# One attention and mixture-of-experts block on one core: how x arrives and is scaled, and the four gate units as seven half-size products

## The chip, the cores and the metric

One NeuronCore of a Trainium2 chip runs the whole program; the other cores are idle. The metric is the device time of one execution in microseconds (us), smaller is better.

## What is computed

All data are float32. `x` is 256 tokens of width 1024. The block adds two terms to it.

```python
h = x
xn = rms_norm(h, norm_mix_g)
proj = xn @ w_in                       # 4808 columns: qa ka va qi ki wi qb kb vb ga gb
# oa: 8 heads over the 64 keys that an index score selects; ob: 8 heads of stick-breaking attention
merged = sigmoid(ga) * (oa @ w_proj_a) + sigmoid(gb) * (ob @ w_proj_b)
h = h + merged @ w_out
hn = rms_norm(h, norm_ffn_g)
# router: top 4 of 32 experts per token; each expert is 1024 -> 2 x 1024 -> 1024 with biases
h = h + sum over the chosen experts of gate * ((up + 1) * g * sigmoid(1.702 * g) @ w_down + b_down)
```

`ga` and `gb` are the two gates, 1024 columns each, so 2048 of the 4808 projected columns. The norm gain multiplies the transposed x by row, the reciprocal root of each token's mean square multiplies it by column.

## The kernel before, in words

**The engines each have one program, written out by hand.** There is no planner: the order on TensorE, VectorE, ScalarE, GpSimd and the DMA queue of SyncE is the order of the calls in the file, and semaphores tie them together. A DMA on SyncE's queue that must wait for a buffer holds all behind it.

**Projection.** `w_in` is cut into ten units (L102): QI, KI with KA, QA, QB, KB, VB, and units 6 to 9, the four gate units of 512 columns. Each is a 2048 KB load. x comes transposed (`XT`, feature chunks of 128 by 256 tokens) in three transfers of 2, 3 and 3 chunks on ScalarE's queue (L1550). VectorE multiplies chunks 0 and 1 by the gain (L1166), ScalarE chunks 2 to 7 (L1556). TensorE's `first_unit` (L652) takes chunk after chunk as they are scaled; behind its chunk 5 come two products that spread the root over the partitions (L648), for which VectorE has to square x (L1169), GpSimd to take the root (L579) and VectorE to build a diagonal from the identity (`ident`, loaded on SyncE's queue, L421), which ends with the semaphore `v_dg` (L1176). A *token half* (L615) is one block of 128 tokens by the unit's columns; a *column half* (L627) is two blocks of 128 columns by all 256 tokens: 16 products of 128x128 by 256 columns, each shown as two records. Results go to the two banks of `Pp`, and ScalarE copies each half out (`evacuate`, L1536, shown as L1544).

**Attention beside it.** Between the halves TensorE does the small products of both attentions (L755 to L796): transposes of the rotated heads (L680; they wait for `v_rota`, with which VectorE ends its normalising and rotating of the A heads, L1213 to L1233), index scores and logits (L697), and for each of four pairs of B heads `b_logits` (L705), `b_sums` (L716, waits for VectorE's `b_softplus`, L1273 and L1276), `b_values` (L725, waits for ScalarE's `b_exp`). The column halves of units 6 to 9 stand between these as work that needs neither VectorE nor GpSimd. `turn_probabilities` (L742) waits for VectorE's `normalise` (L1267).

**GpSimd** does little: a root of 18 numbers per partition (L579), a cast (L587), the router's weights times the gain (L590), all around 50 us, and two more roots later.

**Loads around it.** SyncE loads unit u when the half that frees its buffer is done (L444). Two buffers of 2048 KB (`unit`) serve most units; `w_proj_a`, `w_proj_b` and the two halves of `w_out` are units 10 to 13. Then, after the last attention results (L504), come the first pieces of experts 0 and 1, and after them the experts in order, two experts' places deep, each piece waiting for the release by TensorE (L462).

**After the gates** TensorE multiplies by `w_proj_a` and `w_proj_b` (L809), VectorE merges (L1320), then `w_out` (L820), the router (L837) and 32 experts (L913 to L955), each 12 MB of weights.

Of the kernel before, what the change touches and what calls it, by code (L numbers as in the profile page):

```python
# [21 lines left out]
ALU = mybir.AluOpType  # L22
# [82 lines left out]
GAINS = 5 * KC  # L105

# [30 lines left out]
def hybrid_block(nc, x, xt, w_in, gain_rows, head_rows, w_proj_a, w_proj_b, w_out,  # L137
                 w_router, w_gate_up, b_gate_up, w_down, b_down, consts, out):
    with ExitStack() as ctx:
# [62 lines left out]
        KD = G[:, 0, :, :]  # L202
        RT = OAT[:, 0:3, :]
# [56 lines left out]
        in_xt = [sem(f"in_xt{i}") for i in range(3)]  # L260
# [11 lines left out]
        m_half, a_half = sem("m_half"), sem("a_half")  # L272
        v_roti, v_rota = sem("v_roti"), sem("v_rota")
# [24 lines left out]
        def uview(u, n=512):  # L298
            flat = slot(2, 0, 4096) if u == 2 else unit[:, u % 2, :]
            return flat[:, 0:8 * n].rearrange("p (k n) -> p k n", k=8)  # L300

        def urows(u):

            flat = unit[:, 0, :] if u == 10 else slot(4, 0, 4096)
            return flat.rearrange("p (k n) -> p k n", k=4)

# [97 lines left out]
        def _(sp):  # L404
# [16 lines left out]
            sp.dma_start(ident, consts[:, C_ID:C_ID + P]).then_inc(in_id, 16)  # L421
# [178 lines left out]
        def _(pe):  # L600
# [51 lines left out]
            def first_unit():  # L652

                for k in range(KC):
                    if k < 2:
                        pe.wait_ge(v_xt, k + 1)
                    else:
                        pe.wait_ge(a_xt, k - 1)
# [11 lines left out]
                nhalf[0] = 2  # L670

# [101 lines left out]
            column_half(6, 0)  # L773
# [3 lines left out]
            column_half(6, 1)  # L777
            b_sums(1)
            column_half(7, 0)
# [3 lines left out]
            column_half(7, 1)  # L783
# [3 lines left out]
            column_half(8, 0)  # L787
            b_values(2)
            b_logits(3)
            column_half(8, 1)  # L790
            b_sums(3)
            turn_probabilities(0, 2)
            column_half(9, 0)
            b_values(3)
            a_values(0, 2, 2)
            column_half(9, 1)  # L796
# [4 lines left out]
            for c in range(KC):  # L801
                if c >= 2:
                    pe.wait_ge(v_mg, c - 1)
                else:
                    pe.wait_ge(a_half, nhalf[0] - 1 + c)
# [27 lines left out]
            def router_products(b, i):  # L833

                pe.wait_ge(a_xt, 7 + 2 * b + i)
# [278 lines left out]
        def _(dve):  # L1114
# [49 lines left out]
            dve.wait_ge(in_xt[0], 16)  # L1164
            for k in range(2):
                V.tensor_scalar(XT[:, k, :], XT[:, k, :], g_mix[:, k:k + 1], None, ALU.mult).then_inc(v_xt, 1)  # L1166
# [80 lines left out]

            def select_keys(b, nk):
# [55 lines left out]
            out_of_bank(m_pt, 1, W2, Ap[:, :, :].rearrange("p a n -> p (a n)"), v_pt)  # L1304
            b_softplus(2)
            b_argument(2)
            out_of_bank(m_pv, 1, OAT[:, :, P:SEQ], Ap[:, 0, :].rearrange("p (j q) -> p j q", j=NP2), v_pv)
            mask_logits(0, P, Ap[:, 2:4, :].rearrange("p a (j s) -> p (a j) s", j=NP2), 2)
            b_softplus(3)
            normalise(P, 2)  # L1310
            b_argument(3)
            out_of_bank(m_pt, 2, W2[:, 0:1024], Ap[:, 0:2, :].rearrange("p a n -> p (a n)"), v_pt)
            out_of_bank(m_pv, 2, OAT[:, :, 0:P], Ap[:, 2, :].rearrange("p (j q) -> p j q", j=NP2), v_pv)

# [216 lines left out]
        def _(act):  # L1531
# [18 lines left out]
            for i, (k, n) in enumerate(((0, 2), (2, 3), (5, 3))):  # L1550
                act.dma_start(xt_flat[:, k * SEQ:(k + n) * SEQ], xt[:, k * SEQ:(k + n) * SEQ]).then_inc(in_xt[i], 16)
            act.wait_ge(v_gn, 1)
            for k in range(2, KC):
                if k in (2, 5):
                    act.wait_ge(in_xt[1 if k == 2 else 2], 16)
                A(XT[:, k, :], XT[:, k, :], ACT.Copy, scale=g_mix[:, k:k + 1]).then_inc(a_xt, 1)  # L1556
# [46 lines left out]
            def gate_half(u, hf):  # L1603
                ab, c = (u - 6) // 2, 4 * ((u - 6) % 2) + 2 * hf
                evacuate((G[:, c:c + 2, ab, :], 0, 512, 1.0))
# [12 lines left out]
            gate_half(6, 0)  # L1618
# [3 lines left out]
            gate_half(6, 1)  # L1622
            b_exp(1)
            gate_half(7, 0)
            b_out(1)
            b_log(2)
            gate_half(7, 1)
            b_exp(2)
            gate_half(8, 0)
# [3 lines left out]
            gate_half(8, 1)  # L1633
            b_exp(3)
            gate_half(9, 0)
            b_out(3)
            gate_half(9, 1)
            act.wait_ge(a_half, nh[0])
# [90 lines left out]
```

## Time and profile before

| | us |
|---|---|
| median of 3 runs (1136.64 to 1138.38) | 1138.24 |
| the profiled execution, its own time | 1135.92 |
| its span in the trace | 1134.1 |
| TensorE busy | 1090.9 (96%) |
| VectorE busy | 262.5 (23%) |
| ScalarE busy | 139.7 (12%) |
| GpSimd busy | 8.4 (1%) |
| moved by DMA | 436.69 MB |

The profile divides the span into 40 equal slices of 28.35 us and gives the busy share of each engine in each. A matmul of float32 is two records; the time from group to group in the chain of work is what a group costs, the mean of one record is longer since records overlap.

### The profile page before, as it was taken

Reading aid. Unit: us, or ns where it says so; the run is one execution under the profiler, and the core shown is the slowest. Engines: PE = TensorE matmul, PEld = TensorE weight load, DVE = VectorE, ACT = ScalarE, POOL = GpSimd, SP = SyncE. Lnnn points to the kernel's source line nnn. Section 1 sums busy time; section 2 is a strip of 40 time slices with the busy share of each in tenths; the row PEclk is TensorE's granted clock in tenths of the full one; section 3 lists DMA queues with packets and bytes.
Section 4 is the critical chain, followed back from the end, with each engine's and each line's share of the span. In section 5 each row is a group of like instructions: output and inputs, shape, how many; then the busy total and the mean of one; then the engine's idle time right before and its main releaser. Section 6 shows DMA issues by size and latency. Waiting matters only on the chain.

```text
span 1134.1 us, 11423 instructions
## 1 busy us (share of the span) xinstructions
PE 1090.9 (96%) x5083; PEld 478.5 (42%) x5083; DVE 262.5 (23%) x619; ACT 139.7 (12%) x237; POOL 8.4 (1%) x16
## 2 busy tenths in 40 slices
PE   8999999999999999999999979999999999999997
PEld 5677778443333333333333324333333333333332
DVE  2665323242111111111111111221111111111111
ACT  1415332010000000000000000000000000000001
POOL 0100000000000000000000000000000000000000
PEclk9999999999999999999999998999999999999999
DMA  8365447799999999999999999999999999999996
GB/s 312 156 275 204 189 145 300 296 357 433 431 431 439 431 428 437 435 426 435 428 435 431 428 418 429 427 433 434 431 433 431 432 436 427 431 425 428 428 424 255
DMA packets 21506, 436.69 MB, mean 385 GB/s; under 512 B 2480, under 2 KB 2864, under 8 KB 6384
## 3 DMA queue, kind: packets, MB, share of 16 engines
q1 hardware_dynamic: 20496, 434.22, 90.4%
q10 hardware_dynamic: 960, 1.72, 0.4%
q8 instruction: 41, 0.67, 0.2%
q14 instruction: 9, 0.07, 0.0%
HBM read 434.89 MB, written 1.05 MB: 384 GB/s over the span
## 4 chain that ended last, share of the span: by engine, by line
PE 70%; DMA 24%; DVE 2%; SPq 2%; ACT 1%; issue 0%; ACTq 0%; DVEq 0%
PE Pp L927 31%; DMA gate_up_room<-in_w_gate_up 19%; PE Bp L941 11%; PE Pp L635 7%; PE Ap L955 3%; DMA odd_down<-in_w_down 3%; PE Pp L623 3%; PE Pp L809 2%; PE Ap L820 2%; PE Bp L913 2%; SPq L436 2%; DMA odd_down<-in_b_down 1%; PE Bp L934 1%; DVE odd_down L1457 1%; PE Pp L662 1%; PE Pp L869 1%
## 5 line engine op out<-in xcount | busy, mean ns | idle before, releaser
L927 PE MATMUL Pp<-gate_up_room,OBT 128*64 128x512 f32 x2048 | 453.3, 601 | 17.4 <-DMA gate_up_room<-in_w_gate_up 17.3
L927 PEld LDWEIGHTS Pp<-gate_up_room,OBT 128*64 128x64 f32 x2048 | 147.5, 139 | 307.1 <-issue 279.0
L1446 DVE TENSOR_SCALAR odd_down<-Pp 128x512 f32<-128x512 f32 x31 | 21.4, 692 | 622.2 <-PE Pp L927 622.2
L941 PE MATMUL Bp<-even_down,odd_down 128*64 128x512 f32 x512 | 113.7, 596 | 1.2
L941 PE MATMUL Bp<-odd_down 128*64 128x512 f32 x480 | 106.3, 595 | 1.8 <-DVE odd_down L1457 0.6
L635 PE MATMUL Pp<-odd_down,gate_up_room 128*128 128x256 f32 x384 | 85.2, 381 | 0.0
L1654 ACT ACTIVATE odd_down<-odd_down 128x512 f32<-128x512 f32 x30 | 18.9, 630 | 473.4 <-DVE odd_down L1446 473.4
L635 PEld LDWEIGHTS Pp<-odd_down,gate_up_room 128*128 128x128 f32 x384 | 72.2, 190 | 10.7 <-issue 1.1
L955 PE MATMUL Ap<-odd_down,cst 64*128 64x512 f32 x256 | 64.7, 624 | 4.9 <-DMA odd_down<-in_b_down 4.2
L941 PEld LDWEIGHTS Bp<-even_down,odd_down 128*64 128x64 f32 x512 | 35.2, 137 | 69.0 <-issue 63.3
L941 PEld LDWEIGHTS Bp<-odd_down 128*64 128x64 f32 x480 | 33.2, 137 | 65.3 <-issue 59.9
L913 PE MATMUL Bp<-X,cst 128*64 128x512 f32 x240 | 56.6, 592 | 0.0
L1666 ACT ACTIVATE odd_down<-Bp 128x512 f32<-128x512 f32 x30 | 17.9, 597 | 204.3 <-PE Bp L941 204.3
L955 PEld LDWEIGHTS Ap<-odd_down,cst 64*128 64x128 f32 x256 | 22.3, 187 | 45.4 <-issue 43.9
L623 PE MATMUL Pp<-gate_up_room,odd_down 128*128 128x512 f32 (+1 forms) x96 | 33.5, 508 | 0.0
L1457 DVE COPY odd_down<-Bp 128x512 f32<-128x512 f32 x31 | 21.4, 691 | 44.7 <-PE Bp L934 44.7
L913 PEld LDWEIGHTS Bp<-X,cst 128*64 128x64 f32 x240 | 17.2, 137 | 34.3 <-issue 34.3
L934 PEld LDWEIGHTS Bp<-cst,odd_down 128*128 128x128 f32 x128 | 17.8, 208 | 26.2 <-DVE odd_down L1453 26.2
L820 PE MATMUL Ap<-gate_up_room,odd_down 128*128 128x512 f32 x64 | 28.1, 593 | 0.0
L934 PE MATMUL Bp<-cst,odd_down 128*128 128x128 f32 x128 | 23.7, 308 | 3.2 <-DVE odd_down L1453 3.2
L623 PEld LDWEIGHTS Pp<-gate_up_room,odd_down 128*128 128x128 f32 x96 | 17.4, 190 | 15.1 <-issue 15.0
L1414 DVE TENSOR_TENSOR OBT<-Bp,gains 128x256 f32<-128x256 f32 x62 | 23.1, 411 | 0.0
(209 smaller groups left out, 624.4 us busy)
## 6 DMA issues: line engine op xcount, KB each, us to landing
gate_up_room<-in_w_gate_up SPq DMA_DIRECT2D x27, 2048.0 KB, 42.5
even_down<-in_w_down SPq DMA_DIRECT2D x11, 4096.0 KB, 37.0
odd_down<-in_w_down SPq DMA_DIRECT2D x11, 4096.0 KB, 40.2
gate_up_room<-in_w_gate_up SPq DMA_DIRECT2D x10, 4096.0 KB, 22.0
gate_up_room<-in_w_in SPq DMA_DIRECT2D x8, 2048.0 KB, 7.4
even_down<-in_w_down SPq DMA_DIRECT2D x7, 2048.0 KB, 16.7
odd_down<-in_w_down SPq DMA_DIRECT2D x6, 2048.0 KB, 20.3
odd_down<-in_w_down SPq DMA_DIRECT2D x7, 1024.0 KB, 21.0
```

Source lines behind the costliest of these rows:

```text
L436: sp.dma_start(place(e, i)[:, part], source(e, i)[:, part]).then_inc(done or full(e, i), 16)
L623: last = mm(bank[:, 0:n], XT[:, k, b * P:(b + 1) * P], uview(u, n)[:, k, :], start=k == 0, stop=k == KC - 1)
L635: last = mm(bank[:, t * SEQ:(t + 1) * SEQ], uview(u)[:, k, c:c + P], XT[:, k, :], start=k == 0, stop=k == KC - 1)
L809: last = mm(Pp[:, c % 2, ab * SEQ:(ab + 1) * SEQ], urows(u)[:, j, c * P:(c + 1) * P], o[:, j, :], start=j == 0, stop=j == NP2 - 1)
L820: last = mm(Ap[:, 2 * b + hf, :], XT[:, c, b * P:(b + 1) * P], out_cols(hf)[:, c, :], start=c == 0, stop=c == KC - 1)
L913: last = mm(out_bank[64 * r:64 * r + 64, :], OH[:, b, :], part, start=b == 0, stop=b == 1, skip_group_check=True)
L927: last = mm((Gps, Ups)[q // 2][64 * (q % 2):64 * (q % 2) + 64, :], xT[:, k % 4, k // 4, :], quarter(e, w, q), start=False, stop=k == KC - ...
L934: last = tr(bank[:, c * P:(c + 1) * P], act_fours[:, c, :], ident)
L941: last = mm(bank[64 * hf:64 * hf + 64, :], turned[:, c, s, :], w[:, c * 1024 + hf * 512:][:, 0:512], start=s == 0 and c == 0, stop=s == DN ...
L955: last = mm(Ap[:, 2 * b + hf, :], gates[h, b * P:(b + 1) * P], results[h, :], start=start, stop=stop, skip_group_check=True)
L1414: last = V.tensor_tensor(xT[:, :, r, :], Tps.rearrange("p (c r s) -> p c r s", c=4, r=2)[:, :, r, :], gain[:, 4 * r:4 * r + 4].unsqueeze(2 ...
L1457: V.tensor_copy(hTf, Yps).then_inc(d_ht, 1)
```

## The change

It has two parts.

**x.** The transfers are four, of 1, 1, 3 and 3 chunks. VectorE scales all eight chunks, each group as its transfer lands, ahead of its squares. ScalarE scales none; it does one activation of a single column early. The load of `ident` moves from SyncE's queue to ScalarE's, behind the transfers of x.

**The gate units.** For each of the units 6 to 9 the product (512 columns) by (1024 features) by (256 tokens) is split in two along each, and computed as seven products of half sizes with sums ahead and behind (the Strassen-Winograd form), in place of eight. GpSimd makes the four sums of quarters of XT once (`XS`, 128x512 each) and four sums of quarters of the weights for each unit (128x1024 each). TensorE works on tiles of 128 of the unit's columns, two to a unit, t = 0 to 7: seven products of 4 matmuls of 128x128 by 128 columns each. It takes part sums in PSUM; ScalarE keeps a copy of two of them (128x256), VectorE does a copy and three more operations per tile. TensorE waits for these copies inside a unit, and `v_gate` takes the place of the evacuation semaphore. Unit 6 and unit 9 get a buffer of their own, weight sums take that of `w_out`, and the order of the loads changes.

```diff
+XT_PARTS = ((0, 1), (1, 1), (2, 3), (5, 3))
...
+        XS = norm_pair[:, 0:2048].rearrange("p (s k t) -> p s k t", s=4, k=4)
+        kept = [cst[:, C_ADM:C_ADM + 384], once[:, 1624:2008]]
...
-            flat = slot(2, 0, 4096) if u == 2 else unit[:, u % 2, :]
+            flat = {2: slot(2, 0, 4096), 6: slot(4, 0, 4096), 7: unit[:, 0, :], 8: unit[:, 1, :],
+                    9: slot(4, 0, 4096)}.get(u, unit[:, u % 2, :])
...
-            flat = unit[:, 0, :] if u == 10 else slot(4, 0, 4096)
+            flat = unit[:, u - 10, :]
...
-            sp.dma_start(ident, consts[:, C_ID:C_ID + P]).then_inc(in_id, 16)
...
-            for u in range(11):
+            for u in (0, 1, 2, 3, 4, 6, 5, 7, 8, 9, 10, 11, 12):
                 if u >= 3:
-                    sp.wait_ge(m_half, 4 if u == 3 else 2 if u == 4 else 2 * (u - 1))
+                    sp.wait_ge(m_half, {3: 4, 4: 2, 5: 8, 6: 2, 7: 10, 8: 12, 9: 14, 10: 16, 11: 18, 12: 18}[u])
...
-                if u >= 5 and u < 8:
-                    load_unit(u + 6)
...
             load_half(0, 5, 1)
-            sp.wait_ge(bias_ok, 2)
+            sp.wait_ge(m_half, 20)
+            load_unit(13)
             load_half(1, 5, 0)
-            sp.wait_ge(m_half, 20)
+            load(0, 0)
+            sp.wait_ge(m_mg, KC)
             load(1, 1)
-            sp.wait_ge(m_mg, KC)
-            load(0, 0)
             load_half(0, 5, 0)
             load(1, 0)
...
+            def difference(dst, a, b, op, done):
+                nc.gpsimd.tensor_tensor(dst, a, b, op).then_inc(done, 1)
+
+            pool.wait_ge(v_sx, KC)
+            pool.wait_ge(bias_ok, 2)
+            difference(XS[:, 0], token_quarter(0, 1), token_quarter(0, 0), ALU.subtract, g_xs)
+            difference(XS[:, 2], token_quarter(1, 1), token_quarter(0, 1), ALU.subtract, g_xs)
+            pool.wait_ge(g_xs, 2)
+            difference(XS[:, 1], token_quarter(1, 1), XS[:, 0], ALU.subtract, g_xs)
+            pool.wait_ge(g_xs, 3)
+            difference(XS[:, 3], token_quarter(1, 0), XS[:, 1], ALU.subtract, g_xs)
+            for u in range(6, 10):
+                pool.wait_ge(unit_in[u], 16)
+                if u > 6:
+                    pool.wait_ge(m_half, 6 if u == 7 else 2 * (u - 1))
+                n = 4 * (u - 6)
+                difference(weight_sum(u, 1), weight_quarter(u, 1, 0), weight_quarter(u, 1, 1), ALU.add, g_ws)
+                pool.wait_ge(g_ws, n + 1)
+                difference(weight_sum(u, 2), weight_sum(u, 1), weight_quarter(u, 0, 0), ALU.subtract, g_ws)
+                pool.wait_ge(g_ws, n + 2)
+                difference(weight_sum(u, 4), weight_quarter(u, 0, 1), weight_sum(u, 2), ALU.subtract, g_ws)
+                difference(weight_sum(u, 3), weight_quarter(u, 0, 0), weight_quarter(u, 1, 0), ALU.subtract, g_ws)
...
+            def product(t, part, w, x, start, stop):
+                f = slice(t % 2 * P, t % 2 * P + P)
+                for k in range(4):
+                    last = mm(Pp[:, t % 2, part * P:(part + 1) * P], w[:, k, f], x[:, k, :], start=start and k == 0,
+                              stop=stop and k == 3, skip_group_check=True)
+                return last
+            def gate_products_15(t, u):
+                if t % 2 == 0:
+                    pe.wait_ge(unit_in[u], 16)
+                product(t, 2, weight_quarter(u, 0, 0), token_quarter(0, 0), True, False)
+                if t == 0:
+                    pe.wait_ge(g_xs, 4)
+                if t % 2 == 0:
+                    pe.wait_ge(g_ws, 4 * (u - 6) + 1)
+                product(t, 1, weight_sum(u, 1), XS[:, 0], False, False).then_inc(m_p15, 1)
+            def gate_products_63(t, u):
+                pe.wait_ge(a_p15, t + 1)
+                if t % 2 == 0:
+                    pe.wait_ge(g_ws, 4 * (u - 6) + 3)
+                product(t, 2, weight_sum(u, 2), XS[:, 1], False, False)
+                product(t, 1, weight_sum(u, 4), token_quarter(1, 1), False, True).then_inc(m_p63, 1)
+            def gate_product_7(t, u):
+                pe.wait_ge(v_p6, t + 1)
+                if t % 2 == 0:
+                    pe.wait_ge(g_ws, 4 * (u - 6) + 4)
+                product(t, 2, weight_sum(u, 3), XS[:, 2], False, False).then_inc(m_p7, 1)
+            def gate_products_42(t, u):
+                pe.wait_ge(v_p7, t + 1)
+                product(t, 2, weight_quarter(u, 1, 1), XS[:, 3], False, True)
+                product(t, 0, weight_quarter(u, 0, 1), token_quarter(1, 0), False, True).then_inc(m_half, 1)
...
-            column_half(6, 0)
+            gate_start(6)
             pe.wait_ge(a_half, 12)
             b_values(0)
             b_logits(1)
-            column_half(6, 1)
+            gate_end(6)
             b_sums(1)
...
+            def gate_sum_6(t):
+                dve.wait_ge(m_p63, t + 1)
+                V.tensor_copy(kept[t % 2][:, 2 * P:3 * P], Pp[:, t % 2, 2 * P:3 * P]).then_inc(v_p6, 1)
+            def gate_sum_7(t):
+                dve.wait_ge(m_p7, t + 1)
+                V.tensor_tensor(gate_chunk(t, 1)[:, P:2 * P], kept[t % 2][:, 0:P], Pp[:, t % 2, 2 * P:3 * P],
+                                ALU.add).then_inc(v_p7, 1)
+            def gate_last(t):
+                dve.wait_ge(m_half, 13 + t)
+                V.tensor_copy(gate_chunk(t, 1)[:, 0:P], Pp[:, t % 2, 2 * P:3 * P])
+                V.tensor_tensor(gate_chunk(t, 0), kept[t % 2][:, P:3 * P], Pp[:, t % 2, 0:2 * P], ALU.add)                    .then_inc(v_gate, 1)
...
             select_keys(0, P)
+            gate_sum_6(0)
+            gate_sum_6(1)
+            gate_sum_7(0)
+            gate_sum_7(1)
             b_softplus(1)
+            gate_last(0)
+            gate_last(1)
+            b_argument(1)
             normalise(SEQ, 1)
-            b_argument(1)
...
+            def keep_products(u):
+                for t in (2 * u - 12, 2 * u - 11):
+                    act.wait_ge(m_p15, t + 1)
+                    A(kept[t % 2][:, 0:2 * P], Pp[:, t % 2, P:3 * P], ACT.Copy).then_inc(a_p15, 1)
```

`gate_start(u)` is `gate_products_15` of both tiles and `gate_products_63` of the first (six products of 4 matmuls), each first stage behind `v_gate` of the tile that had the bank before; `gate_end(u)` is `gate_products_63` of the second, `gate_product_7` of both and `gate_products_42` of both (eight). The other three units stand in the same way in the programs of TensorE, VectorE (`gate_sum_6`, `gate_sum_7` and `gate_last` of two tiles each) and ScalarE (`keep_products(u)` behind `b_exp`, in place of the two evacuations).

## Rows read from the trace of the kernel before

**Rows 1.** The page: DMA's busy tenths and rate in 40 slices.

```profile
DMA  8365447799999999999999999999999999999996
GB/s 312 156 275 204 189 145 300 296 357 433 431 431 439 431 428 437 435 426 435 428 435 431 428 418 429 427 433 434 431 433 431 432 436 427 431 425 428 428 424 255
```

**Rows 2.** Windows: busy of PE, PEld, DVE, ACT, POOL, granted clock, DMA share, GB/s.

```profile
300.00:400.00 100.00, 99.66 (x482) 36.36 (x480) 20.49 (x48) 8.83 (x16) 0.00 (x0) 1.00 1.01 433
```

**Rows 3.** Waits of PE from 480 us on, and from 20 to 170 us.

```profile
PE Pp L927 <- DMA gate_up_room<-in_w_gate_up: 17.3, 10, 2.7
...
PE Ap L742 <- DVE gate_up_room L1267: 1.1, 1, 1.1
```

**Rows 4.** SyncE's queue: start, length, what it issues.

```profile
231.81 1.83 SPq L436 DMA_DIRECT2D odd_down<-in_w_down  x2
```

**Rows 5.** The chain that ended last: start, length, work (one row of each kind).

```profile
93.47 6.91 PE Pp L635 x32
...
162.95 7.10 PE Pp L635 x32
...
222.59 1.78 PE Pp L837 x16
```

**Rows 6.** The first 17 us: table load and scaling, TensorE's second stretch, x's squares.

```profile
9.77 1.28 ACT L1556 ACT_TABLE_LOAD   x1 [9.77 <-DMA odd_down<-in_xt]
...
5.88 0.61 DVE L1166 TENSOR_SCALAR odd_down<-odd_down,gains 128x256 f32<-128x256 f32 x2 [1.82 <-DMA odd_down<-in_xt]
...
11.62 7.13 PE L662 MATMUL Pp<-gate_up_room,odd_down 128*128 128x512 f32 x16 [1.63 <-ACT odd_down L1556]
...
14.93 0.22 DVE L1155 SCALAR_TENSOR_TENSOR sm<-sm 128x1 f32<-128x1 f32 x1 [1.34 <-DMA cst<-in_consts]
```

**Rows 7.** ScalarE's copy of 256 columns out of PSUM.

```profile
101.23 0.38 ACT L1595 ACTIVATE OBT<-Bp 128x256 f32<-128x256 f32 x1 [0.21 <-PE Bp L729]
```

**Rows 8.** Around `b_sums(0)`: softplus, `b_sums`, `b_exp`, the end of `select_keys`.

```profile
87.86 0.76 DVE L1276 TENSOR_TENSOR gate_up_room<-gate_up_room,odd_down 128x256 f32<-128x256 f32 x2
...
91.74 0.65 PE Bp L716 x2
...
94.50 0.84 ACT L1591 ACTIVATE gate_up_room<-gate_up_room 128x768 f32<-128x768 f32 x1 [0.83 <-DVE gate_up_room L1282]
...
100.12 0.23 DVE L1254 TENSOR_SCALAR even_down<-even_down 128x128 f32<-128x128 f32 x1
```

**Rows 9.** GpSimd's and VectorE's operations around 12 and 52 us.

```profile
12.37 1.44 POOL L579 TENSOR_TENSOR sm<-sm,odd_down 128x1 f32<-128x1 f32 x1 [11.17 <-DVE sm L1159]
...
12.16 1.23 DVE L1169 CUSTOM_DVE_ANT_0 odd_down<-X 128x1024 f32<-128x1024 f32 x1
...
213.28 0.55 POOL L579 TENSOR_TENSOR sm<-sm,odd_down 128x1 f32<-128x1 f32 x1 [160.21 <-DVE sm L1342]
...
52.45 0.61 POOL L590 TENSOR_TENSOR odd_down<-odd_down,gains 128x256 f32<-128x256 f32 x1
...
52.55 0.54 DVE L1130 TENSOR_TENSOR sm<-sm 128x18 f32<-128x18 f32 x1
...
53.34 0.18 DVE L1132 TENSOR_TENSOR sm<-sm 128x18 f32<-128x18 f32 x1
```

**Rows 10.** VectorE's last operation before `v_rota`, and the chain's row that waits for it.

```profile
58.68 0.36 DVE L1231 COPY odd_down<-gate_up_room 128x128 f32<-128x128 f32 x2
...
67.08 0.59 PE Ap L680 x4
```

**Rows 11.** TensorE after three idle times (the time in brackets) in the expert stage.

```profile
556.90 15.65 PE L927 MATMUL Pp<-gate_up_room,OBT 128*64 128x512 f32 x64 [2.50 <-DMA gate_up_room<-in_w_gate_up]
...
585.96 13.95 PE L927 MATMUL Pp<-gate_up_room,OBT 128*64 128x512 f32 x64 [0.78 <-DMA gate_up_room<-in_w_gate_up]
...
676.78 3.05 PE L955 MATMUL Ap<-odd_down,cst 64*128 64x512 f32 x8 [4.21 <-DMA odd_down<-in_b_down]
```

**Rows 12.** The page, DMA issues: number, KB each, median us to landing.

```profile
gate_up_room<-in_w_in SPq DMA_DIRECT2D x8, 2048.0 KB, 7.4
```

More of the change, by code:

```diff
@@ L259, in hybrid_block @@
         first_in = [sem(f"first_in{i}") for i in range(5)]
-        in_xt = [sem(f"in_xt{i}") for i in range(3)]
+        in_xt = [sem(f"in_xt{i}") for i in range(len(XT_PARTS))]
         one_ok, v_dg, m_rb, m_first, v_sx = (sem(n) for n in ("one_ok", "v_dg", "m_rb", "m_first", "v_sx"))
@@ L272, in hybrid_block @@
         m_half, a_half = sem("m_half"), sem("a_half")
+        g_xs, g_ws = sem("g_xs"), sem("g_ws")
+        m_p15, m_p63, m_p7 = sem("m_p15"), sem("m_p63"), sem("m_p7")
+        a_p15, v_p6, v_p7, v_gate = sem("a_p15"), sem("v_p6"), sem("v_p7"), sem("v_gate")
         v_roti, v_rota = sem("v_roti"), sem("v_rota")
@@ L298, in uview, with weight_quarter, weight_sum, token_quarter @@
         def uview(u, n=512):
-            flat = slot(2, 0, 4096) if u == 2 else unit[:, u % 2, :]
+            flat = {2: slot(2, 0, 4096), 6: slot(4, 0, 4096), 7: unit[:, 0, :], 8: unit[:, 1, :],
+                    9: slot(4, 0, 4096)}.get(u, unit[:, u % 2, :])
             return flat[:, 0:8 * n].rearrange("p (k n) -> p k n", k=8)
         def urows(u):
-            flat = unit[:, 0, :] if u == 10 else slot(4, 0, 4096)
+            flat = unit[:, u - 10, :]
             return flat.rearrange("p (k n) -> p k n", k=4)
+        def weight_quarter(u, f, k):
+            return uview(u)[:, 4 * k:4 * k + 4, 256 * f:256 * f + 256]
+        def weight_sum(u, i):
+            return slot(u % 2 * 2, 1024 * (i - 1), 1024).rearrange("p (k n) -> p k n", k=4)
+        def token_quarter(k, b):
+            return XT[:, 4 * k:4 * k + 4, b * P:(b + 1) * P]
+        def gate_chunk(t, f):
+            u = 6 + t // 2
+            return G[:, 4 * (u % 2) + t % 2 + 2 * f, (u - 6) // 2, :]
         def out_cols(hf):
@@ new lines, in gate_products_42, with gate_start @@
+            def gate_products_42(t, u):
+                pe.wait_ge(v_p7, t + 1)
+                product(t, 2, weight_quarter(u, 1, 1), XS[:, 3], False, True)
+                product(t, 0, weight_quarter(u, 0, 1), token_quarter(1, 0), False, True).then_inc(m_half, 1)
+            def gate_start(u):
+                a, b = 2 * u - 12, 2 * u - 11
+                if u == 6:
+                    pe.wait_ge(a_half, 11)
+                else:
+                    pe.wait_ge(v_gate, a - 1)
+                gate_products_15(a, u)
+                if u == 6:
+                    pe.wait_ge(a_half, 12)
+                else:
+                    pe.wait_ge(v_gate, a)
+                gate_products_15(b, u)
+                gate_products_63(a, u)
@@ L672, in _, with gate_end @@
+            def gate_end(u):
+                a, b = 2 * u - 12, 2 * u - 11
+                gate_products_63(b, u)
+                gate_product_7(a, u)
+                gate_product_7(b, u)
+                gate_products_42(a, u)
+                gate_products_42(b, u)
             first_unit()
@@ L1163, in _ @@
             dve.wait_ge(v_gn, 1)
-            dve.wait_ge(in_xt[0], 16)
-            for k in range(2):
-                V.tensor_scalar(XT[:, k, :], XT[:, k, :], g_mix[:, k:k + 1], None, ALU.mult).then_inc(v_xt, 1)
+            for i, (k0, n) in enumerate(XT_PARTS):
+                dve.wait_ge(in_xt[i], 16)
+                for k in range(k0, k0 + n):
+                    V.tensor_scalar(XT[:, k, :], XT[:, k, :], g_mix[:, k:k + 1], None, ALU.mult).then_inc(v_xt, 1)
             for b in range(TB):
@@ L1300, in _ @@
             select_keys(0, P)
+            gate_sum_6(0)
+            gate_sum_6(1)
+            gate_sum_7(0)
+            gate_sum_7(1)
             b_softplus(1)
+            gate_last(0)
+            gate_last(1)
+            b_argument(1)
             normalise(SEQ, 1)
-            b_argument(1)
+            gate_sum_6(2)
             out_of_bank(m_pt, 1, W2, Ap[:, :, :].rearrange("p a n -> p (a n)"), v_pt)
+            gate_sum_6(3)
+            gate_sum_7(2)
+            gate_sum_7(3)
             b_softplus(2)
+            gate_last(2)
+            gate_last(3)
             b_argument(2)
@@ L1308, in _ @@
             mask_logits(0, P, Ap[:, 2:4, :].rearrange("p a (j s) -> p (a j) s", j=NP2), 2)
+            gate_sum_6(4)
+            gate_sum_6(5)
+            gate_sum_7(4)
+            gate_sum_7(5)
             b_softplus(3)
+            gate_last(4)
+            gate_last(5)
             normalise(P, 2)
@@ L1312, in _ @@
             out_of_bank(m_pt, 2, W2[:, 0:1024], Ap[:, 0:2, :].rearrange("p a n -> p (a n)"), v_pt)
+            gate_sum_6(6)
             out_of_bank(m_pv, 2, OAT[:, :, 0:P], Ap[:, 2, :].rearrange("p (j q) -> p j q", j=NP2), v_pv)
+            gate_sum_6(7)
+            gate_sum_7(6)
+            gate_sum_7(7)
+            gate_last(6)
+            gate_last(7)
             for c in range(KC):
@@ L1549, in _ @@
             xt_flat = XT.rearrange("p k t -> p (k t)")
-            for i, (k, n) in enumerate(((0, 2), (2, 3), (5, 3))):
+            for i, (k, n) in enumerate(XT_PARTS):
                 act.dma_start(xt_flat[:, k * SEQ:(k + n) * SEQ], xt[:, k * SEQ:(k + n) * SEQ]).then_inc(in_xt[i], 16)
[L1552 to L1556, printed above, removed]
+            act.dma_start(ident, consts[:, C_ID:C_ID + P]).then_inc(in_id, 16)
+            act.wait_ge(p_half, 1)
+            A(sm[:, 158:159], mhalf[:, 0:1], ACT.Copy)
             def evacuate_keys(b):
@@ L1617, in _ @@
             b_exp(0)
-            gate_half(6, 0)
+            keep_products(6)
             b_out(0)
```

36 lines of the change are left out of this document (13 added, 23 removed).

## The prediction

> **What bounds the kernel now.** I read the page first: the DMA rate rises to some 430 GB/s in the ninth slice and stays there to the end, with uneven slices before [rows 1]. The windows say the same: from 300 to 400 us the DMA share is 1.01 and TensorE is busy for 99.66 of 100 us [rows 2]. In the expert stage TensorE is a little faster than the loads: from 480 us on it waits ten times, 17.3 us, for expert weights [rows 3]. So the end is set by a stream of weights that never pauses once it is full. It is full from about 232 us, when SyncE issues the last halves for expert 1 behind the router and the ranks [rows 4]. All of these issues wait for TensorE, and the transfers in the gaps before are the same bytes before and after the change. So what TensorE gains or loses ahead of 232 us moves the start of the full stream, and the end, one for one. A faster expert stage would give nothing, a faster attention stage gives all.
>
> Ahead of 232 us TensorE is the bound: between 20 and 170 us it hardly waits (1.1 us for `normalise` is the longest) [rows 3], and the chain goes over its products [rows 5]. The question is what its 76.6 us from `b_sums`' end at 93.47 to the gates' end at 170.06 (162.95 + 7.10) become [rows 5], and whether something new holds it earlier.
>
> **The start.** TensorE's second stretch begins at 11.62, 1.63 us after its first ended, since x's second transfer landed at about 9.7 and ScalarE then loaded a table for 1.28 us ahead of its first scaling [rows 6]. VectorE needs 0.31 us for a chunk (0.61 for two) [rows 6]: 9.7 + 0.31 + 0.04 = 10.05, a gain of 1.57. Against it: one more issue on ScalarE's queue may land that transfer up to 0.5 later. The squares now stand behind eight scalings, but they no longer wait for `ident`, which held VectorE until 14.93 [rows 6]; I get `v_dg` at about 17.2, and TensorE comes to its two root products at 17.2. Between 0.6 and 1.6 I take **−1.2**.
>
> **The gate products.** Before: eight column halves of 6.91 or 7.10 us, five of one and three of the other, 55.9 us [rows 5]. After: 8 tiles x 7 products x 4 matmuls of 128x128 by 128 columns. The router's products have this form: 16 records, that is 8 matmuls, in 1.78 us [rows 5], so 0.89 for four. 56 x 0.89 = 49.8, **−6.1**. I walked through the waits with the durations of the rows. A copy out of PSUM by ScalarE is 0.38 for 256 columns [rows 7]; on VectorE 256 columns are 0.42 or less (two in 0.76 [rows 8]), so by the line 0.3 for 128; a tile costs VectorE 0.3 + 0.3 + 0.3 + 0.4 = 1.3 us, all eight 10.4. Each copy is asked for one product (0.89) or more after its source is ready, the tiles go by turns, and VectorE's long `select_keys` ends at 100.35 [rows 8], while in the same count TensorE wants the first copy behind it at 102.8 (93.5 + 5.3 for six products + 2.2 for `b_values` and `b_logits` + 1.8 for two). The cover for `b_sums` to `b_values` shrinks from 6.9 to six products, 5.3; `b_exp` is done at 94.50 + 0.84 = 95.34 [rows 8], 1.9 behind `b_sums`. The wait for `normalise` of the last block stays at about 1 us. So the terms here are −6.1, with 0 to +1 for a copy that comes late.
>
> **GpSimd and VectorE get in each other's way.** GpSimd's new sums are tensor operations with two inputs in SBUF. The trace shows what such neighbours do. A root of one column takes GpSimd 0.55 us alone (213.28), but 1.44 at 12.37, beside VectorE's square of 1.23, which has two inputs too and ran from 12.16 to 13.39 [rows 9]. The other way round, VectorE's product of 18 columns takes 0.18 alone (53.34), but 0.54 from 52.55, beside GpSimd's 0.61 from 52.45: both end within 0.03 us of each other [rows 9]. They go by turns, and the one that is late waits for the whole of the other's operation. This is where the new work falls: directly behind the router's weights at 53.06 GpSimd does four sums of 512 columns and the four of unit 6, since unit 6 is loaded early. At that time VectorE is in the chain that ends with `v_rota`: 18 operations from 53.1 to 59.04, nearly all with two inputs (one of the first, and the last: [rows 9, 10]). TensorE needs `v_rota` at 67.08 [rows 10], a slack of 8.0.
>
> The size: 256 columns are 0.61 [rows 9]. If all of it grows with the columns, 1024 are 2.45 and 512 are 1.23; with 0.1 fixed, 2.15 and 1.12. Taking 2.3 and 1.17, eight operations are 4 x 1.17 + 4 x 2.3 = 13.9 us. VectorE has more than eight places between its dependent operations, so all eight get in. From each I take off 0.25, since a blocked VectorE operation ended only 0.03 after GpSimd's (0.15 of its start lies beside it) and GpSimd's start does the same: 13.9 − 2.0 = 11.9. `v_rota` comes at 70.9, and TensorE stands for **+3.8**. Bounds: 0 (nothing shared for these forms, or VectorE first each time: up to 8 us are free) and 14.7 − 8.0 = +6.7.
>
> The Trainium skill, SBUF — State Buffer, section "Who interferes with whom", has the rule that the two engines share one pair of ports and the later one is blocked fully. Taken as the whole length with no overlap, the wait would be 13.9 − 8.0 = 5.9 in place of 3.8, and my sum would be 2.1 us higher.
>
> **The clock.** After 0.78 us of idleness 64 matmuls took 13.95, after 2.50 they took 15.65; after 4.21 us eight took 3.05, 0.38 each where the first case has 0.22 [rows 11]. An idle time of 3.8 us falls among those that are followed by work at the lower clock, 1.2 GHz in place of 2.4, and the price of one is 15.65 − 13.95 = 1.7 us, at four chances in five or so: **+1.5**; bounds 0 and 2.
>
> **A second meeting.** Unit 7's weight sums begin when its load has landed, 7.4 us in the median [rows 12], up to 10, after the half that ends at 75.26 before. That puts them from 83 on, and VectorE's two-input part of the softplus stands at 87.86, 3.1 us ahead of the `b_sums` at 91.74 which wait for it [rows 8]. One GpSimd operation in the way (2.3) is covered, two are not: 0 to 1 here, and as much again for the first copy, since the rest of VectorE's row moves too. I take **+0.7**. Units 8 and 9 meet `normalise` at most, which has 4 us to spare. The moved loads cost nothing: `w_out`'s second half is behind 7 MB, lands at about 180 and is asked for at about 200.
>
> **Sum:** −1.2 − 6.1 + 3.8 + 1.5 + 0.7 = **−1.3 us**. The profiled execution took 1135.9 and would take 1134.6; it lies 2.3 below the median, and the forecast for the median is 1138.2 − 1.3 = 1136.9. What a measurement of this kernel can tell from no change is 0.2%, 2.3 us.
>
> **Rivals.**
> - *No turn-taking that matters.* If the new operations do not block VectorE before `v_rota`, or by less than the slack of 8.0, three terms fall away: −1.2 − 6.1 = −7.3, 1130.9. For it: the evidence on blocking is three short operations. Against it: they all show it, in both directions. 0.27.
> - *GpSimd is slower, and TensorE stands at `v_rota` for long.* If a sum of 1024 columns takes 3.3 us (strided quarters, hand-overs) and one of 512 takes 1.65, the eight are 19.8, less 2.0 is 17.8, the wait 9.8; with 1.7 for the clock and 2 for the second meeting the sum is +6.2, 1144.4. The kernel is slower by over 0.2% once this wait passes some 7.4 us. For it: only one row prices such a sum, of a quarter of the size. Against: that row is not alone with itself, VectorE was already there. 0.14. By the Trainium skill, GPSIMD Engine Reference, section "3.1 Elementwise — side-by-side cycle accounting", a sum of 2048 takes 4.5 us; half of it, an estimate, is my 2.3 and speaks against this rival.
> - *It does not reach the end.* The stream starts earlier, but the loads' rate and not its start sets the end, for instance by more competition in the gaps: change about 0, 1138. Against: the share is 1 from 240 us on with nothing left to take up a shift. 0.07.
>
> **How the numbers follow.** The forecast has 0.52; its own range is −4 to +2, for the length of the wait and whether the clock falls: 1134.2 to 1140.2. With the rivals the range is 1130.4 to 1141.0. Faster by over 2.3: the first rival and a third of the forecast, 0.43. Slower by over 2.3: the second and 0.03 of the forecast, 0.17. Within: 0.40.
>
> **What would show it.** In the changed trace: TensorE's second stretch at 10 to 10.5 us; VectorE's operations between 53 and 70 us with 1 to 2.5 us each in place of 0.2 to 0.8; the chain naming VectorE's line of `v_rota`, with TensorE idle for about 4 us and a granted clock under 1 behind it; four matmuls of a gate product in 0.89; the gates' end some 1.3 us earlier than 170.06, and the first expert by the same. If TensorE has no gap before the gates, the first rival holds. If it has gaps inside the gates, my walk through the copies was wrong.

## The result and the profile after

The changed kernel takes 1141.34 us in the median of 10 runs (1139.26 to 1143.08), the kernel before 1137.6 in 10 runs beside it. The ratio is 1.0033, 95% interval 1.0022 to 1.0043: slower by 3.7 us, where I had forecast 1.3 us less. The profiled execution took 1139.73, its span 1137.9, 3.8 more than before.

The chain that ended last in the changed kernel (start us, length us, work; "issue" is time for which the profile names nothing that was waited for) shows where:

```profile
16.98 31.50 issue
...
48.51 3.24 POOL sm L598
...
70.59 0.37 DVE odd_down L1335 x2
...
71.01 1.12 PE Ap L783 x4
...
73.40 8.55 PE Pp L677 x32
81.96 6.87 PE Pp L665 x16
88.82 0.63 PE Bp L808 x4
...
106.05 2.05 PE Pp L715 x16
...
174.01 27.63 PE Pp L912 x128
```

L598 is GpSimd's root, L579 of before. L783 and L1335 are L680 and L1231 of before, L677 is the column half L635, L665 the token half L623, L808 is L705, L715 the new products, L912 is L809. The chain now runs through GpSimd's root and VectorE's operations up to `v_rota`; before, it stayed on TensorE from 22 to 101 us. Against before:

| mark | before | after | later by | this stretch alone |
|---|---|---|---|---|
| GpSimd's root of 18 begins | 48.91 | 48.51 | −0.40 | −0.4 |
| transposes behind `v_rota` begin | 67.08 | 71.01 | +3.93 | +4.3 |
| `b_logits(0)` begins | 82.09 | 88.82 | +6.73 | +2.8 |
| `b_sums(0)` begins | 91.74 | 99.3 | +7.6 | +0.9 |
| gates' end | 170.06 | 174.01 | +3.95 | −3.6 |
| first expert's products begin | 236.08 | 240.04 | +3.96 | 0 |
| span | 1134.1 | 1137.9 | +3.8 | −0.2 |

The waits of TensorE from 20 to 260 us (engine, line, what it waited for, us, times, longest) have three that the kernel before does not have: at `v_rota`, inside the first gate unit (L715), and at `b_sums(0)` (L819).

```profile
PE Ap L783 <- DVE odd_down L1335: 4.3, 1, 4.3
...
PE Pp L715 <- ACT cst L1750: 1.2, 1, 1.2
...
PE Bp L819 <- DVE gate_up_room L1397: 0.8, 1, 0.8
```

**The chain on VectorE.** First GpSimd's new operations of that time, then VectorE's beside them, from the timeline (start, length, engine, line, operation):

```profile
52.61 6.12 POOL L613 TENSOR_TENSOR odd_down<-odd_down 128x512 f32<-128x512 f32 x4
58.69 10.22 POOL L613 TENSOR_TENSOR gate_up_room<-gate_up_room 128x1024 f32<-128x1024 f32 x4
89.29 9.69 POOL L613 TENSOR_TENSOR gate_up_room<-gate_up_room 128x1024 f32<-128x1024 f32 x4 [20.38 <-DMA gate_up_room<-in_w_in]
```

```profile
53.95 1.19 DVE L1235 TENSOR_TENSOR sm<-sm 128x18 f32<-128x18 f32 x1
...
58.84 2.81 DVE L1330 TENSOR_TENSOR gate_up_room<-gate_up_room,sm 128x576 f32<-128x576 f32 x1
61.69 2.72 DVE L1331 TENSOR_TENSOR gate_up_room<-gate_up_room,odd_down 128x512 f32<-128x512 f32 x1
64.33 2.37 DVE L1332 TENSOR_TENSOR gate_up_room<-gate_up_room,odd_down 128x64 f32<-128x64 f32 x1
66.73 2.35 DVE L1246 TENSOR_TENSOR even_down<-gate_up_room,odd_down 128x144 f32<-128x144 f32 x1
```

The operation of 64 columns at 64.33 takes 2.37 us, the one of 512 ahead of it 2.72. The same operations in the kernel before (timeline):

```profile
54.34 0.69 DVE L1227 TENSOR_TENSOR gate_up_room<-gate_up_room,odd_down 128x512 f32<-128x512 f32 x1
54.96 0.22 DVE L1228 TENSOR_TENSOR gate_up_room<-gate_up_room,odd_down 128x64 f32<-128x64 f32 x1
```

So neither length is its own: most of each is one GpSimd operation of 1024 columns, of which the shortest took 2.33 us. The product of 18 columns took 0.18 before [rows 9] and 1.19 now. From 69.0 on, GpSimd being done, the same kinds are back at 0.22 and 0.31.

**The clock.** Granted clock at the end of the wait and behind it (window, busy PE, clock, DMA share, GB/s):

```profile
69.00:70.00 1.00, 0.00 (x0) 0.89 0.00 0
70.00:71.00 1.00, 0.00 (x0) 0.50 0.00 0
...
72.00:73.00 1.00, 1.00 (x7) 0.50 0.00 0
...
76.00:77.00 1.00, 1.00 (x4) 0.70 0.00 0
77.00:78.00 1.00, 1.00 (x6) 1.00 0.00 0
```

The granted clock fell at about 69.8, while TensorE still stood, and was back at full at about 76.6. From 71.0 to 76.6, 5.6 us, TensorE worked at 1.2 GHz without a gap. That lengthened the transposes and the column half behind them, which took 8.55 us where it took 6.91 before [rows 5].

### The profile page after: what moved, and what is told of

Its sections match the earlier page's. It is cut to its first block, busy times and chain, and to the rows that moved or that the text cites. A ratio compares the mean times of both kernels' runs of the same rounds, so it can differ in the third digit from the quotient of the medians.

```text
span 1137.9 us, 11873 instructions
## 1 busy us (share of the span) xinstructions
PE 1089.0 (96%) x5275; PEld 480.9 (42%) x5275; DVE 291.3 (26%) x657; ACT 135.6 (12%) x232; POOL 54.6 (5%) x36
## 4 chain that ended last, share of the span: by engine, by line
PE 66%; DMA 20%; DVE 5%; issue 4%; SPq 3%; ACT 1%; POOL 0%; ACTq 0%; DVEq 0%; POOLq 0%
PE Pp L1030 32%; DMA gate_up_room<-in_w_gate_up 15%; PE Bp L1044 12%; PE Pp L715 4%; PE Ap L1058 3%; DMA odd_down<-in_w_down 3%; PE Bp L1016 3%; SPq L457 2%; PE Pp L912 2%; PE Ap L923 2%; PE Bp L1037 1%; DMA odd_down<-in_b_down 1%; DVE odd_down L1602 1%; DMA odd_down<-in_xt 1%; PE Pp L972 1%
## 5 line engine op out<-in xcount | busy, mean ns | idle before, releaser
L1030 PE MATMUL Pp<-gate_up_room,OBT 128*64 128x512 f32 x2048 | 452.2, 600 | 13.9 <-DMA gate_up_room<-in_w_gate_up 13.9
L715 PE MATMUL Pp<-odd_down,gate_up_room 128*128 128x128 f32 x448 | 52.2, 276 | 1.2 <-ACT cst L1750 1.2
L715 PEld LDWEIGHTS Pp<-odd_down,gate_up_room 128*128 128x128 f32 x448 | 50.8, 192 | 2.6 <-ACT cst L1750 1.3
L613 POOL TENSOR_TENSOR gate_up_room<-gate_up_room 128x1024 f32<-128x1024 f32 x16 | 40.3, 2531 | 46.8 <-PE Pp L715 25.8
L665 PE MATMUL Pp<-gate_up_room,odd_down 128*128 128x512 f32 (+1 forms) x96 | 33.5, 507 | 0.0
L677 PE MATMUL Pp<-odd_down,gate_up_room 128*128 128x256 f32 x128 | 29.9, 396 | 0.0
L677 PEld LDWEIGHTS Pp<-odd_down,gate_up_room 128*128 128x128 f32 x128 | 25.4, 200 | 4.0 <-issue 0.3
```

The source lines that it names most:

```text
L613: nc.gpsimd.tensor_tensor(dst, a, b, op).then_inc(done, 1)
L665: last = mm(bank[:, 0:n], XT[:, k, b * P:(b + 1) * P], uview(u, n)[:, k, :], start=k == 0, stop=k == KC - 1)
L677: last = mm(bank[:, t * SEQ:(t + 1) * SEQ], uview(u)[:, k, c:c + P], XT[:, k, :], start=k == 0, stop=k == KC - 1)
L715: last = mm(Pp[:, t % 2, part * P:(part + 1) * P], w[:, k, f], x[:, k, :], start=start and k == 0, stop=stop and k == 3, skip_group_check= ...
L1030: last = mm((Gps, Ups)[q // 2][64 * (q % 2):64 * (q % 2) + 64, :], xT[:, k % 4, k // 4, :], quarter(e, w, q), start=False, stop=k == KC - ...
```

## The experiments

The kernel before ran beside each: 1137.17 us (22 runs) beside x alone, gates alone, the unused sums and the three waits; 1136.3 (34) beside the writes, the filled wait, the first wait only and x in three transfers; 1137.96 (12) beside the last kernel. So ratios, not medians, compare between groups.

| kernel | gates' end, us | median, us | ratio to before, 95% |
|---|---|---|---|
| changed | 174.01 | 1141.34 | 1.0033 (1.0022 to 1.0043) |
| x alone | 169.88 | 1136.61 | 0.9993 (0.998 to 1.0006) |
| gates alone | 173.50 | 1141.65 | 1.004 (1.0027 to 1.0053) |
| before + unused sums | 176.75 | 1143.52 | 1.0052 (1.0037 to 1.0067) |
| before + writes | 169.65 | 1138.05 | 1.0012 (0.9999 to 1.0025) |
| changed + filled wait | 171.96 | 1137.96 | 1.0015 (1.0003 to 1.0027) |
| changed + first wait only | 167.36 | 1133.84 | 0.9978 (0.9963 to 0.9993) |
| changed + three waits | 164.31 | 1131.45 | 0.9947 (0.9932 to 0.9963) |
| the same, x in three transfers | 164.85 | 1131.73 | 0.996 (0.9947 to 0.9973) |
| the same, x as before | 166.32 | 1131.71 | 0.995 (0.9929 to 0.9971) |

### The two parts, each alone

`x_alone` is the kernel before with the diff's lines on `XT_PARTS`, `v_xt` and `ident`; `gates_alone` is the changed kernel with these undone.

> The kernel before with the new way of x alone (four transfers, all eight chunks scaled by VectorE, ident on ScalarE's queue). In the changed kernel all marks behind the start stood 0.4 us earlier than before, so if the two parts add up this one gives 0.4 us less than the kernel before. A rival: the parts do not add up, because VectorE's later squares cost more without the gates' slack; then it is 0 to 1 us slower.

> The changed kernel with x as before: seven products, GpSimd's sums where the change put them. If the parts add up it takes 4.2 us more than the kernel before (3.8 of the two profiles plus the 0.4 of x). TensorE stands about 4.3 us at v_rota. If instead x's later arrival makes the wait at v_rota, the wait is gone here and the kernel is 3 us faster than before.

x alone is 0.6 us faster in the median and its interval holds 1. The gates alone are 4.5 us slower, and TensorE waits 4.3 us at `v_rota` again. So the loss is the gates', and x's arrival has no hand in the wait. The first rows of x in the changed kernel (timeline):

```profile
8.14 0.35 DVE L1270 TENSOR_SCALAR odd_down<-odd_down,gains 128x256 f32<-128x256 f32 x1 [2.33 <-DMA odd_down<-in_xt]
...
10.43 0.88 DVE L1270 TENSOR_SCALAR odd_down<-odd_down,gains 128x256 f32<-128x256 f32 x3 [1.94 <-DMA odd_down<-in_xt]
10.84 7.13 PE L701 MATMUL Pp<-gate_up_room,odd_down 128*128 128x512 f32 x16 [0.31 <-DVE odd_down L1270]
12.70 0.88 DVE L1270 TENSOR_SCALAR odd_down<-odd_down,gains 128x256 f32<-128x256 f32 x3 [1.40 <-DMA odd_down<-in_xt]
```

TensorE goes on at 10.84, not at 11.62 [rows 6]. But the last chunks land at 12.7, the squares wait for them, and the root products come at 18.08 where they came at 18.59. And the start itself is not that repeatable: GpSimd's root of 18 numbers begins at 48.50, 48.91, 49.10, 49.28 and 50.48 in the five profiled kernels with x's old way, and at 48.48 to 48.99 in five with the new one. So the 0.4 us between the two profiles is not shown to be x's doing.

### The price of the sums alone

```diff
+            pool.wait_ge(v_sx, KC)
+            pool.wait_ge(bias_ok, 2)
+            difference(XS[:, 0], token_quarter(0, 1), token_quarter(0, 0), ALU.subtract)
...
+            difference(XH[:, 0], XT[:, 0:4, :], XT[:, 4:8, :], ALU.add)
...
```

These are eight sums, four of 512 and four of 1024 columns, behind the router's weights. The loads and the merge that reuse their places also wait for them, 90 us or more later.

> The kernel before with eight sums on GpSimd that nobody uses, four of 512 and four of 1024 columns, in the place where the change has its first eight; nothing else is changed. The theory: v_rota comes about 12 us later, TensorE stands 4.3 us and works at the lower clock for some 5 us behind it, and the time is 7 us over the kernel before. The rival (the sums as such cost nothing, the loss is in the rest of the change): the time of the kernel before within 1 us.

Measured: 1143.52, ratio 1.0052. Nothing of the Strassen form is in this kernel, and it has the wait and the slow column half (waits of TensorE, then the chain):

```profile
PE Ap L709 <- DVE odd_down L1260: 4.6, 1, 4.6
```

```profile
72.03 0.88 PE Ap L709 x4
...
74.19 7.73 PE Pp L664 x32
```

The rival falls: the eight operations cost 6.3 us of medians by themselves (5.9 by the ratio), in the trace 4.6 in the wait and 1.7 in the clock (from the transposes to the end of the column half 9.89 us, against 8.15 before).

### Writes in place of sums

```diff
+            for i in range(18):
+                if i:
+                    pool.wait_ge(g_extra, i)
+                nc.gpsimd.memset(norm_pair[:, 1024 * (i % 2):1024 * (i % 2) + 1024], 0.0).then_inc(g_extra, 1)
```

> The kernel before with 18 memsets of 1024 columns on GpSimd, one behind the other, from 53 us on, some 16 us: GpSimd is busy as long as with the eight unused sums, but reads nothing. If the turn-taking is about the second input that VectorE reads, VectorE's chain keeps its times, and the kernel takes the time of the one before within 1 us. The rival (any large operation of GpSimd blocks VectorE): v_rota late by about 12 us and 6 us over the kernel before, as with the sums.

GpSimd is busy for 18 us in the same place, and VectorE's operations with two inputs keep their lengths; two lines with one input do not (timeline of this kernel):

```profile
52.58 18.13 POOL L600 MEMSET odd_down<- 128x1024 f32 x18
```

```profile
52.71 0.85 DVE L1140 TENSOR_SCALAR sm<-sm 128x18 f32<-128x18 f32 x1
53.60 0.18 DVE L1141 TENSOR_TENSOR sm<-sm 128x18 f32<-128x18 f32 x1
...
54.60 0.69 DVE L1236 TENSOR_TENSOR gate_up_room<-gate_up_room,odd_down 128x512 f32<-128x512 f32 x1
...
58.94 0.79 DVE L1240 COPY odd_down<-gate_up_room 128x128 f32<-128x128 f32 x2
```

`v_rota` comes at 59.73, TensorE does not wait there, and the ratio is 1.0012, with an interval (0.9999 to 1.0025) that just holds 1. So it is not GpSimd's being busy that costs. What the memsets leave out is the reading, and without it VectorE's second input is not held up. The Trainium skill, SBUF — State Buffer, section "Who interferes with whom", says both: an operation of VectorE with two inputs in SBUF contends with one of GpSimd that reads SBUF, not with one that only writes it, while scalings and copies can run in a mode that takes the shared ports and can then contend with GpSimd. These rows agree: 0.18 and 0.69 for two inputs, as without the memsets, 0.85 for a scaling that takes 0.18 otherwise, and 0.79 for two copies that take 0.36 [rows 10].

### The wait kept, the clock kept up

```diff
+            for _ in range(18):
+                mm(Bp[:, 1, 0:P], XT[:, 0, 0:P], XT[:, 0, 0:P], start=True, stop=True, skip_group_check=True)
             pe.wait_ge(v_rota, 1)
```

> The changed kernel with 18 products of 128x128 by 128 columns, whose results nobody uses, between the last index scores and the wait for v_rota: 4.0 us of work for TensorE in the 4.3 us in which it stood. The theory: v_rota comes as late as before, but the granted clock stays at 1 behind it, and the 2.8 us that the clock cost are saved; the gates end at about 171.2 and the time is 2.8 under the changed kernel's 1141.3, 1138.5. The rival (the slow stretch behind v_rota has another cause, such as GpSimd's reads beside TensorE's): the time of the changed kernel.

Timeline of TensorE, and a window behind the wait:

```profile
66.99 4.29 PE L866 MATMUL Bp<-odd_down 128*128 128x128 f32 x36
71.41 0.66 PE L783 MATMUL Ap<-cst,gate_up_room 128*128 128x128 f32 x4
...
72.56 7.07 PE L677 MATMUL Pp<-odd_down,gate_up_room 128*128 128x256 f32 x32
```

```profile
73.00:75.00 2.00, 2.00 (x11) 1.77 (x10) 1.86 (x5) 0.00 (x0) 0.00 (x0) 1.00 0.00 0
```

`v_rota` is as late as in the changed kernel (its transposes begin at 71.41, all marks of this profile being 0.4 later), and the column half is back at 7.07, which is also its length in this view before. The gates' end is 2.05 us earlier though its start was 0.4 later. The rival falls; the clock was worth 2 to 3 us of the 3.7.

How long the slow stretch lasts varies. From the transposes to the end of the column half the changed kernel took 10.95 us, the gates alone 9.83 and the unused sums 9.89, against 8.15 before, so it cost 2.8, 1.7 and 1.7. In the gates alone the clock fell only as TensorE began again, at about 71.5, and was down for 3.4 us:

```profile
71.00:72.00 1.00, 0.41 (x2) 0.76 0.00 0
...
74.00:75.00 1.00, 1.00 (x3) 0.54 0.00 0
```

In the changed kernel it was down for 6.8 us, 5.6 of them under work. Why the clock fell earlier in one of them is open. Each is a single profiled execution, so the 2.8 is that of one execution, and the ratios do not show the changed kernel slower than the gates alone.

### GpSimd's sums where nobody waits beside them

```diff
+            pool.wait_ge(v_sum, 1)
             pool.wait_ge(v_sx, KC)
...
+                if u == 7:
+                    pool.wait_ge(v_bs, 1)
+                if u == 8:
+                    pool.wait_ge(v_pr, 1)
                 n = 4 * (u - 6)
```

> The changed kernel with three waits added on GpSimd alone: the sums of x and of unit 6 begin behind VectorE's index_scores(1), unit 7's behind the first softplus, unit 8's behind the first normalise. No sum then runs beside a two-input operation of VectorE that anybody waits for. The theory (turn-taking of GpSimd and VectorE makes the loss): no wait at v_rota, granted clock 1 throughout, no wait at b_sums(0), unit 6's first copy in time; the gates end at 170.06 - 0.4 - 4.6 - 0.2 = 164.9, and the kernel takes 5 us less than the kernel before, 9 less than the changed one. The rival (the staged products and their copies make the loss): the wait at v_rota moves into the gates, since the weight sums come later; at best the time of the kernel before.

> The changed kernel with the first of the three waits alone (the sums of x and unit 6 behind index_scores(1)); units 7 and 8 as in the change. The theory: no wait at v_rota and no fall of the clock, but the second meeting stays: softplus(0)'s two operations take 4 us or more in place of 0.8, b_sums(0) is 0.8 late and the first copy of unit 6 1.2 late. Some 2 us over the kernel with all three waits, 1133.5. The rival (that meeting comes only from the first one's delay): no difference to all three waits.

In `quiet` GpSimd waits three times: the sums of x and unit 6 stand behind the last of VectorE's index scores (`v_sum`), those of unit 7 behind the first softplus (`v_bs`), those of unit 8 behind the first `normalise` (`v_pr`). `quiet_first` has the first of these waits alone. The kernel with three waits takes 1131.45 us, 5.7 less than the kernel before, with the same products, copies and load order as the changed one. GpSimd in it, and the chain:

```profile
62.79 5.18 POOL L613 TENSOR_TENSOR odd_down<-odd_down 128x512 f32<-128x512 f32 x4 [10.16 <-DVEq L1355]
67.93 9.55 POOL L613 TENSOR_TENSOR gate_up_room<-gate_up_room 128x1024 f32<-128x1024 f32 x4
88.35 9.55 POOL L613 TENSOR_TENSOR gate_up_room<-gate_up_room 128x1024 f32<-128x1024 f32 x4 [10.88 <-DVE gate_up_room L1402]
```

```profile
66.64 0.59 PE Ap L788 x4
...
93.04 5.36 PE Pp L720 x48
...
100.61 7.34 PE Pp L720 x64
...
164.31 15.76 PE Pp L917 x73
```

Eight sums take 14.7 us here and 16.3 in the changed kernel: GpSimd too waits for its turn. TensorE has no gap at `v_rota` or `b_sums(0)`. With the first wait alone the gates' end is 3.0 us later, 0.5 of which is a later start: the softplus meets unit 7's sums, as in the changed kernel (timeline of the kernel with the first wait alone).

```profile
87.94 4.66 DVE L1398 TENSOR_TENSOR gate_up_room<-gate_up_room,odd_down 128x256 f32<-128x256 f32 x2
```

Two operations without a wait between them took 0.76 before [rows 8] and 4.66 here, twice one of GpSimd's: it gets in between even these. `b_sums(0)` is 0.8 late. VectorE's masking of the logits and `b_argument` follow, so ScalarE's `b_exp` and its copy of unit 6's products behind it are late as well: the 1.2 us of L716, the L715 of the changed kernel. With what TensorE loses by beginning again inside the six products, the stretch from the end of `b_sums(0)` to `b_values(0)` takes 7.07 us in the changed kernel and 5.36 with three waits, 1.7 more. This second meeting takes place whether or not the first one did.

### x once more

`quiet_three` is that kernel with `XT_PARTS = ((0, 2), (2, 3), (5, 3))`; `quiet_gates_alone` has x as before.

> The kernel with all three waits, and x in three transfers of 2, 3 and 3 chunks, all scaled by VectorE. The four transfers landed at 5.4, 8.1, 10.4 and 12.7 us, so one fewer should bring the third chunk at 9.2 to 9.7 in place of 10.4 and the last at about 12. Expected 0.5 to 0.9 us less than with four, 1130.8. The rival: the arrival of all of x is set by its bytes, so that v_dg and with it TensorE's root products come when they came: the same time.

> The kernel with all three waits on GpSimd, and x as in the kernel before (three transfers, ScalarE scaling six chunks). It tells what the way of x is worth once nothing else is lost: the x part alone gave a ratio of 0.9993, 0.6 us of medians, so 5.2 us less than the kernel before, ratio 0.9954. The rival: the x part is worth what I had predicted (1.2 us) and the way it overlaps hid it; then the ratio is 0.996 or more, beside 0.9947 with the new x.

The ratios are 0.996 and 0.995; each interval holds the other's value and the 0.9947 of four transfers. With three transfers the last chunks land at 12.1 and `v_dg` comes at 17.43 in place of 18.02, the 0.6 us that was expected. TensorE's root products still come at 18.70 in this profile, against 18.05 to 18.57 with four, but here the granted clock was down from about 7.9 to 11.1 while TensorE worked:

```profile
7.00:8.00 1.00, 1.00 (x3) 0.92 1.00 301
8.00:9.00 1.00, 1.00 (x3) 0.50 1.02 398
```

That costs half of 3.2 us, so this profile does not tell what three transfers give TensorE, and the ratios do not show a gain. With x as before, root products and gates' end are 2 us later in the profile than with the new way of x (20.16, and 166.32 against 164.31), but the medians are 1131.71 and 1131.45. What the way of x is worth lies below what these runs can tell; that it is worth 0.4 us is neither shown nor excluded.

## Why the prediction was wrong

Its mechanism was the right one, place by place, and the sum had the wrong sign, because all five of its terms were too favourable. They add up to −1.3; what the traces show in their places adds up to −0.4 − 5.3 + 4.3 + 2.8 + 2.5 = +3.9, beside +3.95 at the gates' end and +3.7 in the medians. The steps that failed most are the two terms for what hangs on the wait, the second meeting (+0.7 for 2.5) and the clock (+1.5 for 2.8).

- **The start, forecast −1.2, measured −0.4.** The step "one more issue on ScalarE's queue may land that transfer up to 0.5 later" priced a cut transfer as an issue alone. The four transfers landed at 5.4, 8.1, 10.4 and 12.7 us. The last one holds up the squares and so `v_dg` (18.02, not 17.2), and with it the root products. The measured 0.4 is itself no more than profiles of one way of x differ among themselves.
- **The gate products, forecast −6.1.** Four matmuls in 0.89 holds inside a stretch: 5.36 us for six products. The last stretch of a unit, eight products, is 7.34, not 7.12, and one stretch of six is 5.55: in some places the beginning costs 0.2 more, as it did in the column halves of 7.10, and the chain has four such. In the kernel with three waits the stretch from `b_sums(0)`'s end (93.04) to the gates' end is 71.27 against 76.59 before, −5.3; in the changed one, with the late copy, −3.6 from `b_sums(0)` on. I had the walk through the copies right: no copy was late by the gates' own doing.
- **The wait at `v_rota`, forecast +3.8, measured +4.3.** The step was right in its count (eight turns, all of them before `v_rota`) and nearly in its size: VectorE's chain grew by 12.3 us, forecast 11.9. One undisturbed operation of 1024 columns takes 2.33 to 2.36 us, forecast 2.3, and one of 512 takes 1.27, forecast 1.17. The reading with no overlap, 13.9, gives 5.9 for this wait; the trace lies between, nearer the overlap.
- **The clock, forecast +1.5 with a bound of 2, measured +2.8.** I took the price, 1.7, from one case and put the bound close above it. The price was right for two kernels, the gates alone and the unused sums; in the profiled execution of the changed one, behind the same wait, it was 2.8, since there the clock was down from before TensorE began again until 76.6. The row of 4.21 us [rows 11] would not have given more for its own stretch: the clock was down from 677.6 to 681.0 there, 3.4 us, which is 1.7 again. But it fell a second time at about 684.7 and stayed down for some 10 us, and a bound of 2 had no room for a longer stretch.
- **The second meeting, forecast +0.7, measured +0.8 at `b_sums(0)` and +1.7 at the first copy** (1.2 of wait, the rest for beginning again). Both places were named, as "0 to 1 here, and as much again for the first copy". I took a third of a range whose upper end was the case in which GpSimd gets in between two operations, and that is what it does.
- **One for one to the end** held: +3.95 at the gates, +3.96 at the first expert, +3.8 in the span. Over all the kernels the span behind the gates' end is 963.5 to 968.4 us. These 4.9 us are more than the effect, so one pair of profiles would not show it, but in every kernel the change of the gates' end and the change that the ratio gives agree within 2 us, from −6 to +6.

The rivals: "no turn-taking that matters" is what the kernel with three waits makes true, and its time, 5.7 under the kernel before, is near the 7.3 that I gave it. "GpSimd is slower" is refuted by 2.36 us for an operation where it wanted 3.3. The range, up to 1141.0, failed at its upper end: it let the wait, the clock and the second meeting be dear one at a time, though TensorE pays for each of them: the clock hangs on the wait, and the second meeting comes on its own.

## What to carry to other kernels

Before moving elementwise work to an idle GpSimd, look at what VectorE does in that stretch: in these traces a sum on GpSimd made a two-input operation of VectorE wait for nearly its whole length, in turns. So the bill was the number of GpSimd's operations that fitted in the chain times most of their length: eight of them, 14.7 us alone, cost 12.3, and two of 2.36 cost 3.9. VectorE's busy share does not tell it. Place such work behind a semaphore that says that the chain has passed; here three waits on GpSimd turned 3.7 us lost into 5.7 won, with nothing else changed. And price a gap of several us on TensorE with the slow work behind it, not only by its length.

## What the runs showed of the hardware that I had not expected

- GpSimd also gets between two VectorE operations that follow each other without a wait: 4.66 and 4.67 us for a pair that takes 0.76.
- A memset of 1024 columns on GpSimd (1.0 us) left VectorE's two-input products alone, but made a scaling of 18 columns take 0.85 in place of 0.18 and two copies 0.79 in place of 0.36.
- Transfers of 128 KB and of 384 KB on ScalarE's queue landed 2.3 to 2.9 us apart alike (once 3.6), beside the weights on SyncE's queue. Cutting the first transfer in two brought its first half at 5.1 to 5.8 us in place of 5.9 to 6.5, and chunk 2 at 10.3 to 10.9 in place of 9.1 to 9.8.
- The same wait of 4.3 us was followed by slow work that cost 1.7 us in one kernel and 2.8 in another: in the first the granted clock fell as TensorE began again and was down for 3.4 us, in the other it fell 1.2 us before that and was down for 6.8.
